# Dealing an expert's ranks to the 64 row slots in steps of eight

## The reference, cut to what matters

```python
gi = jnp.argmax(gl, axis=-1)                       # one of 4 groups
vals, idx = lax.top_k(sel, TOP_K_IN_GROUP)         # two of its 8 experts
eid = gi[:, None] * EXPERTS_PER_GROUP + idx        # 2 of 32 experts per token
for e in range(N_EXPERTS):
    he = jax.nn.silu(tok @ p['w_exp_gate'][e]) * (tok @ p['w_exp_up'][e])
    y = y + combine[:, e:e + 1] * (he @ p['w_exp_down'][e]).astype(jnp.float32)
```

## Time and profile before

| | us |
|---|---|
| median of 3 runs | 1062.22 (1059.92 to 1065.66) |
| the profiled execution | 1060.58 |
| its span, first to last instruction | 1058.8 |
| PE busy in the span | 930.8 (88%) |
| POOL busy | 331.2 (31%) |
| expert stage, last step of gate and up starts | 1005.4 |

### The profile page before, as it was taken

One profiled execution on the slowest core, in us unless ns is written; L12 is line 12 of the kernel. 1 busy time (PEld: TensorE's weight loads), 2 busy tenths in 40 slices (PEclk: granted clock), 3 DMA queues, 4 the chain that ended last, 5 costly groups with the idle time before them and its releaser, 6 DMA issues.

```text
span 1058.8 us, 14529 instructions
## 1 busy us (share of the span) xinstructions
PE 930.8 (88%) x5865; PEld 625.1 (59%) x5878; DVE 395.4 (37%) x754; ACT 295.0 (28%) x484; POOL 331.2 (31%) x276
## 2 busy tenths in 40 slices
PE   3999998899998999999989999999988988989840
PEld 3789998896997988897743443344333333333310
DVE  4301188825642247778742122221212112211118
ACT  1463433352575478351311000000000000001111
POOL 7555476770433344650001111111111111112112
PEclk9999999999999999999779999999999999999985
DMA  9961544447676763385848999999999999999841
GB/s 322 327 135 48 105 106 109 80 100 229 194 155 210 159 239 130 116 298 238 343 189 342 425 426 424 426 424 426 424 425 426 427 425 427 426 425 424 348 156 53
DMA packets 60822, 294.15 MB, mean 278 GB/s; under 512 B 7525, under 2 KB 9165, under 8 KB 48162
## 3 DMA queue, kind: packets, MB, share of 16 engines
q1 hardware_dynamic: 49296, 272.68, 69.4%
q0 software_dynamic: 6560, 11.47, 3.1%
q10 hardware_dynamic: 4914, 9.28, 2.4%
HBM read 290.23 MB, written 14.68 MB: 288 GB/s over the span
## 4 chain that ended last, share of the span: by engine, by line
PE 53%; DMA 28%; DVE 9%; ACT 4%; issue 3%; POOL 1%; SPq 1%; POOLq 0%; ACTq 0%; DVEq 0%
DMA ring<-in_w_exp_up 18%; PE bank L1454 15%; PE bank L1477 6%; PE bank L1106 6%; PE bank L1108 5%; PE bank L1107 5%; DMA ring<-in_w_in 5%; DMA cond_slot<-in_w_cond 4%; PE bank L1057 1%; PE bank L1444 1%; PE bank L1047 1%; DVE hf L1967 1%; PE bank L1466 1%; DVE out_lo L1785 1%; ACT hf L958 1%
## 5 line engine op out<-in xcount | busy, mean ns | idle before, releaser
L1454 PE MATMUL bank<-ring,hf 128*64 128x512 f32 x1024 | 229.5, 601 | 19.4 <-DMA ring<-in_w_exp_up 18.4
L549 POOL TENSOR_TENSOR w_lo<-ring,w_hi 128x1024 fp32r<-128x1024 f32 x76 | 183.8, 2430 | 168.5 <-ACT w_hi L771 168.5
L1106 PE MATMUL bank<-h_hi,w_hi 128*128 128x320 f32 x576 | 183.6, 319 | 7.9 <-POOL w_lo L549 6.7
L1108 PE MATMUL bank<-h_hi,w_lo 128*128 128x320 f32 x576 | 178.7, 310 | 0.0
L1454 PEld LDWEIGHTS bank<-ring,hf 128*64 128x64 f32 x1024 | 78.3, 139 | 167.0 <-issue 153.6
L1477 PE MATMUL bank<-ring,he 128*64 128x512 f32 x512 | 127.2, 642 | 0.6 <-DVE he L1971 0.5
L1107 PE MATMUL bank<-h_lo,w_hi 128*128 128x320 f32 x384 | 119.3, 311 | 0.0
L1106 PEld LDWEIGHTS bank<-h_hi,w_hi 128*128 128x128 f32 x576 | 108.8, 189 | 14.6 <-issue 10.1
L608 POOL DMA_INDIRECT xrow<-expert_inputs,sidx x32 | 32.8, 1024 | 256.1 <-DVE sidx L1957 234.2
L1108 PEld LDWEIGHTS bank<-h_hi,w_lo 128*128 128x128 f32 x576 | 108.8, 189 | 0.0
L1967 DVE TENSOR_TENSOR hf<-hf,bank 64x512 f32<-64x512 f32 x32 | 22.1, 690 | 230.8 <-ACT hf L958 230.8
(11 more groups left out here) (380 smaller groups left out, 1301.3 us busy)
## 6 DMA issues: line engine op xcount, KB each, us to landing
ring<-in_w_exp_gate SPq DMA_DIRECT2D x32, 2048.0 KB, 27.7
ring<-in_w_exp_down SPq DMA_DIRECT2D x32, 2048.0 KB, 31.6
ring<-in_w_exp_up SPq DMA_DIRECT2D x32, 2048.0 KB, 32.2
ring<-in_w_in SPq DMA_DIRECT2D x15, 2048.0 KB, 13.8
cond_slot<-in_w_cond SPq DMA_DIRECT2D x9, 2048.0 KB, 11.5
ring<-in_w_cond SPq DMA_DIRECT2D x3, 2048.0 KB, 18.7
ring<-in_w_branch_b SPq DMA_DIRECT2D x2, 2048.0 KB, 8.5
ring<-in_w_branch_a SPq DMA_DIRECT2D x2, 2048.0 KB, 9.6
```

What stands on the lines that cost most here:

```text
L549: pool.tensor_tensor(w_lo_of[slot][:, :, c], raw[:, :, c], w_hi[:, :, c].bitcast(F32), ALU.subtract)\
L1106: mm(b, hi[:, k, c], x_hi[:, k, :], start=(k == 0), stop=False)
L1108: last = mm(b, lo[:, k, c], x_hi[:, k, :], start=False, stop=(k == KT - 1))
L1454: last = mm(bank[1][64 * q:64 * q + 64, :], xg[:, k % 4, k // 4, :], ring[s + q][:, k * FF:k * FF + FF], start=(k == 0), stop=(k == KT - 1 ...
```

## The change

The two halves of `slot_iota` no longer hold 0, 1, 2, ..., 63 (less 10000) but, for slot 8i+j, the number i+8j. The rank of a token no longer equals the number of its slot: ranks 0 to 7 sit in slots 0, 8, 16, ..., 56, ranks 8 to 15 in slots 1, 9, ..., 57, and so on. Everything that follows takes the slots as they come; the scatter uses the same indices, so results go to the same rows of DRAM.

```diff
@@ -516,7 +516,7 @@
                 ch.add(pool.tensor_copy(dst, iota_i[:, 0:width]))
 
             for c in range(2):
-                iota(slot_iota[:, c * SLOTS:(c + 1) * SLOTS], SLOTS, [[1, SLOTS]], -int(FAR), 0)
+                iota(slot_iota[:, c * SLOTS:(c + 1) * SLOTS], SLOTS, [[1, 8], [SLOTS // 8, 8]], -int(FAR), 0)
             for t in range(3):
                 iota(e_iota[:, t, :], E, [[1, E]], 0, 0)
                 iota(g_iota[:, t, :], NG, [[1, NG]], 0, 0)
```

## The result

| | before | after |
|---|---|---|
| median, 20 runs each, us | 1062.84 (1056.51 to 1067.87) | 1066.05 (1062.71 to 1072.76) |
| ratio, 95% interval | | 1.0037 [1.0022, 1.0052] |
| profiled execution and span, us | 1060.58, 1058.8 | 1068.1, 1066.3 |

The changed kernel is slower by 0.37%, 3.9 us (2.3 to 5.5), against a forecast of +4.1 us. These microseconds are taken from the ratio, which is an estimate over all runs; the two medians alone differ by 3.2 us. The program gives every engine the same instructions in the same order, so all of it is in when things happen.

The account below looks back on a forecast made before the run. Bound: the slowest DMA engine's total bytes in the expert stage. 4.0 + 0.1 = +4.1 us on 1060.58 gives 1064.7; with the median 1.6 us higher, 1066.3, rounded to 1066 us; range 1063 to 1069, widened to 1060 to 1070.

Parts of the forecast that it names:

- The stage ends with the slowest of 16 equally fast queues: Expert stage: DMA engines always busy from 590 to 990 us; the slowest ends about 1010.2 us, 16 us behind the first.
- Strips of four: Gathers and scatters: engine k has slots 4k to 4k+3 and 32+4k to 35+4k; 242 to 24 rows per engine.
- blocks of eight: Alternative slot assignment, slots 8k to 8k+7 per engine: 441 to 0 rows, a spread of 34 us before the change.
- every eighth slot: Alternative slot assignment to engines: 173 to 119 rows, a spread of 4 us, no step before 1006 us.
- Eight partitions in a row: Rival for engine load: worst engine falls from 441 to 173 rows, -21 us, about 1042 us; chance 0.05.
- The change loads eight engines: End of weight traffic: load on the even engines, share near 0.5 from some 20 us before the end.
- The term of +4.0 us: Slowest engine's gathers and scatters: 242 to 295 rows, packets 20.05 to 24.08 us; last up chunk +4.0 us, lowest bound +3.4.
- A half-filled packet costs half: Gather and scatter packets: 158 ns with both slots filled, 85 ns with one, 9 ns empty; the price of bytes.
- rival 3: Even engines' queues: a half-filled packet costs a turn, not its bytes; +8.0 us, 1070 us; chance 0.11.
- Gathers hidden, iota hidden: Gathers would need 5.8 us more to be late; iotas at most 0.4 of 1.55 us GpSimd wait; both taken as 0.
- Issue to landing grows by a few us: Expert weight chunks: time from issue to landing, 33 to 38 us before, would grow by a few us.
- The tail keeps its 53.5 us: From the last up chunk's landing to the end: fixed tail keeps its 53.5 us; last scatter +0.08 us.

Follow-up runs that it names:

- the packed deal: Against the kernel before: an engine's eight slots (two strips of four) filled before the next engine gets any; 1078.68 us, ratio 1.0168.
- the even deal: Against the kernel before: single ranks dealt so that ranks 0 to 7 go to eight different strips of four slots; 1057.67 us, ratio 0.9949.
- the pairs: Against the kernel before: the same even strips filled as in the change, but neighbouring ranks share a packet; 1064.51 us, ratio 1.0034.

## Why the prediction was right, point by point

- *The stage ends with the slowest of 16 equally fast queues.* Shown: four deals of the same bytes, with the slowest at 173, 198, 242 and 441 rows, came out in that order at -5.4, -3.3, 0 and +17.8 us, and the plateau runs at 424 to 427 GB/s before and at 423 to 427 after the change. The two deals at 295 and 310 rows lie between the last two, at +3.9 and +3.6 us, too near to each other for the times to order them. How far the last engine lies behind the mean agrees with the packet sums within 1.1 us in all profiles but that of the packed deal (20.4 against 22.2).
- *Strips of four.* Shown by three kernels together. On the packed deal and on the change itself, blocks of eight have the opposite sign; on the even deal, every eighth slot has. The section on the descriptor swizzle in the Trainium skill (DMA: Bandwidth & Descriptors) has the same strips, stated for a 1 MiB transfer to 128 partitions. The trace agrees, and here the transfers are indirect ones of 128 half rows. Eight partitions in a row does not agree.
- *The change loads eight engines.* Shown by the half share from 996 to 1012 us.
- *The term of +4.0 us.* The time came out as forecast: +3.9 us by the ratio twice (3.2 and 3.5 us between the medians). The term itself is smaller in the traces: in both profiles of the changed kernel the last engine lies further behind the mean by 2.8 to 2.9 us, not by 4.0, which is under the lowest of the bounds (3.4). The 4.0 us by which expert 30's chunk landed later in the first profile hold over 1 us of a stage that began later. The runs' interval (2.3 to 5.5 us) holds 2.9 as well as 4.0, so that the forecast met the time within 0.2 us is in part luck. What makes up the rest, if there is one, is open: the longer tail below may be a part of it.
- *A half-filled packet costs half.* That it doesn't cost a full one is shown by the 85 ns of the earlier trace rows, by the time of the change, whose +8.0 us by rival 3 lie outside the 2.3 to 5.5 us measured, and by the sign of the pairs in the traces. The packets themselves take 159, 85 and 9 ns in the trace of the changed kernel as well. That an engine falls behind by just that is not shown: the changed kernel, which has the most half-filled packets on its slowest engine, came out 0.8 us under its packet sum and the pairs in its strips 1.1 us over theirs.
- *Gathers hidden, iota hidden.* No wait of TensorE for a gather is in the chain. The two iotas take 0.21 us in place of 0.19, on an engine that goes on to wait.
- *Issue to landing grows by a few us.* Wrong. From 600 to 1010 us, in the changed kernel against the earlier trace rows:

```profile
ring<-in_w_exp_gate SPq DMA_DIRECT2D x26, 2048.0 KB, 33.3
ring<-in_w_exp_up SPq DMA_DIRECT2D x26, 2048.0 KB, 37.6
```

A chunk is issued when the buffer of three experts earlier is free, so both ends of the interval are delayed alike; that is read off the program. The number says how deep the ring is, not how late the queue.
- *The tail keeps its 53.5 us.* Wrong in both profiles of the changed kernel, by 2.3 us in the first and 1.6 us in the second (55.0 us from 1007.37 to 1062.4), with 1.7 us of each the last down product, partly at the lower clock. There is one profile of the kernel before to compare with, so it is not shown whether the other executions of that kernel have the shorter tail too.

## What to carry to other kernels

When a stage sits on a full DMA plateau, look at how it ends: a share that falls in steps is a measure of how unevenly the engines are loaded, and the more engines stand idle for long, the more an even deal can give, up to where another engine paces the stage. Find from that staircase which partitions an engine serves before you redistribute anything; a deal that is even by the wrong grouping is worse than none. The kernel to keep is the even deal over strips of four, 0.5% faster than before; in its profile TensorE runs the last three steps without waiting for a chunk, so the next step there would have to be TensorE's.

## What the runs showed that I had not expected

Whether TensorE's last down product ran partly at the lower granted clock (5.35 us) or at the full one (3.65 us) went with whether TensorE had waited for the last chunk: it had in the kernel before (0.41 us) and in the packed deal (0.85 us), both at the full clock, and not in the other seven profiles, all of which show about 5.4 us. So 1.7 us of what an earlier chunk saves may be given back there. But the link doesn't hold one step earlier, as the packed deal itself shows:

```profile
986.78 7.09 PE L1454 MATMUL bank<-ring,hf 128*64 128x512 f32 x32 [1.41 <-DMA ring<-in_w_exp_up]
...
996.57 5.35 PE L1477 MATMUL bank<-ring,he 128*64 128x512 f32 x16
...
1018.36 7.09 PE L1454 MATMUL bank<-ring,hf 128*64 128x512 f32 x32 [0.85 <-DMA ring<-in_w_exp_up]
...
1028.06 3.65 PE L1477 MATMUL bank<-ring,he 128*64 128x512 f32 x16 [0.52 <-DVE he L1971]
```

After a wait of 1.41 us the down product took 5.35 us, after one of 0.85 us it took 3.65. It is mostly one profile of each kernel and nothing was tried on it; the link may be chance, and the cause is open.
